# Shifting every buffer of split weights by 192 bytes against the other matmul operands

## What is computed

```
for l in range(2):
    z = rms_norm(x) @ w_in[l]            # 1024 -> 5632: u | q | k | v | two gates
    y_a = s5_branch(u);  y_a = gelu(y_a);  y_a *= sigmoid(y_a @ w_glu[l] + b)
    y_b = rms_norm(diff_attention(rope(q), rope(k), v))
    m = sigmoid(g_ssm) * (y_a @ w_proj_ssm[l]) + sigmoid(g_attn) * (y_b @ w_proj_attn[l])
    x = x + m @ w_out[l]
    h = rms_norm(x)
    x = x + (swiglu(h) if l == 0 else top2_of_8_experts(h))   # hidden width 2816
return rms_norm(x)
```

## Time and profile before

| | before |
|---|---|
| median of 2 runs | 1452.74 us (1451.63 to 1453.85) |
| span of the profiled execution | 1453.1 us |
| TensorE matmul busy (PE) | 1426.3 us, 98% |
| VectorE busy (DVE) | 1179.7 us, 81% |
| ScalarE busy (ACT) | 884.7 us, 61% |
| read from HBM | 390.98 MB |

### The profile page before, as it was taken

The page is one execution under the profiler, slowest core; times in us unless marked ns, Lnnn a source line. Parts: engine busy times, 40 slices in busy tenths (PEclk is TensorE's granted clock), DMA queues, the critical chain, the costliest instruction groups (busy, mean ns, idle before and its releaser), DMA issues.

```text
span 1453.1 us, 22261 instructions
## 1 busy us (share of the span) xinstructions
PE 1426.3 (98%) x8381; PEld 1202.9 (83%) x8381; DVE 1179.7 (81%) x1181; ACT 884.7 (61%) x879; POOL 141.4 (10%) x195
## 2 busy tenths in 40 slices
PE   8999999999999999999999999999999999999997
PEld 6887888999998888887888888888888888888875
DVE  7998886676467697876988988889898898898896
ACT  5334754534344345644768768777777777777774
POOL 1910100000000000101960000000000000000100
PEclk9999999999999999999999999999999999999999
DMA  7443445776455442454999999999999999999993
GB/s 285 136 180 121 156 159 189 261 246 233 151 189 192 174 160 97 151 188 161 365 413 390 406 363 399 380 364 413 353 398 394 354 404 370 379 397 347 419 376 145
DMA packets 94247, 408.87 MB, mean 281 GB/s; under 512 B 28769, under 2 KB 43233, under 8 KB 47714
## 3 DMA queue, kind: packets, MB, share of 16 engines
q1 hardware_dynamic: 75984, 391.37, 69.9%
q10 hardware_dynamic: 17042, 12.36, 2.6%
q0 software_dynamic: 1152, 4.19, 0.7%
HBM read 390.98 MB, written 14.16 MB: 279 GB/s over the span
## 4 chain that ended last, share of the span: by engine, by line
PE 78%; DVE 11%; DMA 3%; SPq 3%; issue 2%; ACT 2%; POOL 1%; DVEq 0%; POOLq 0%; ACTq 0%
PE psum L1938 25%; PE psum L1940 24%; PE psum L1939 24%; DVE w_lo L605 4%; SPq L696 3%; PE psum L1954 2%; DMA w_raw<-in_stream 2%; DMA x_normed<-y_rows,row_number 1%; ACT w_hi L599 1%; ACT square_out L993 0%; PE psum L2284 0%; PE psum L2005 0%; DVE s_r L1511 0%; ACT prob L1129 0%; PE psum L1987 0%
## 5 line engine op out<-in xcount | busy, mean ns | idle before, releaser
L605 DVE TENSOR_TENSOR w_lo<-w_raw,w_hi 128x2048 fp32r<-128x2048 f32 x267 | 607.9, 2293 | 130.2 <-ACT w_hi L599 129.4
L599 ACT ACTIVATE w_hi<-w_raw 128x2048 fp32r<-128x2048 f32 x267 | 509.4, 1915 | 251.1 <-PE psum L1940 191.5
L1938 PE MATMUL psum<-w_hi,hsT_hi 128*128 128x512 f32 x448 | 176.0, 393 | 0.8 <-DVE hsT_lo L1829 0.8
L1940 PE MATMUL psum<-w_lo,hsT_hi 128*128 128x512 f32 x448 | 174.5, 390 | 0.0
L1939 PE MATMUL psum<-w_hi,hsT_lo 128*128 128x512 f32 x448 | 174.3, 389 | 0.0
L1938 PE MATMUL psum<-w_hi,hT_hi 128*128 128x512 f32 x376 | 152.7, 406 | 1.8 <-ACT gate_ssm L1075 1.4
L605 DVE TENSOR_TENSOR w_lo_more<-w_raw,w_hi_more 128x2048 fp32r<-128x2048 f32 x56 | 128.2, 2289 | 24.3 <-ACT w_hi_more L599 23.6
L1940 PE MATMUL psum<-w_lo,hT_hi 128*128 128x512 f32 x376 | 147.4, 392 | 0.0
L1939 PE MATMUL psum<-w_hi,hT_lo 128*128 128x512 f32 x376 | 147.1, 391 | 0.0
L599 ACT ACTIVATE w_hi_more<-w_raw 128x2048 fp32r<-128x2048 f32 x56 | 107.1, 1913 | 21.6 <-DMA w_raw<-in_stream 12.4
L1938 PE MATMUL psum<-hT_hi,w_hi 128*128 128x256 f32 x416 | 116.6, 280 | 0.2 <-DVE hT_lo L1463 0.2
(11 more groups left out here) (429 smaller groups left out, 2651.2 us busy)
## 6 DMA issues: line engine op xcount, KB each, us to landing
w_raw<-in_stream SPq DMA_DIRECT2D x323, 1024.0 KB, 6.9
w_raw_more<-in_stream SPq DMA_DIRECT2D x40, 1024.0 KB, 7.7
h_rows<-one_row ACTq DMA_DIRECT2D x10, 512.0 KB, 6.6
round_rows<-h_rows SPq DMA_DIRECT2D x7, 512.0 KB, 7.0
y_rows<-y_slots ACTq DMA_DIRECT2D x7, 512.0 KB, 9.2
y_rows<-one_row ACTq DMA_DIRECT2D x4, 512.0 KB, 6.2
gain_row<-in_gain_rows SPq DMA_DIRECT2D x3, 512.0 KB
x_tok<-in_x SPq DMA_DIRECT2D x2, 512.0 KB, 6.2
```

Of the source, the lines that this page charges most:

```text
L599: nc.scalar.activation(split_of(seg, i)[0], raw_of(seg, i), ACT.Copy).then_inc(s_hi, 1)
L605: nc.vector.tensor_tensor(l_, raw_of(seg, i), h.bitcast(F32), ALU.subtract).then_inc(s_lo, 1)
L1938: mm(out, lh, rh, start=start, stop=False)
L1940: return mm(out, lh, rl, start=False, stop=stop)
```

## The change

All split weights get the lead, in all segments. `LEAD` becomes a tuple with one entry for each of the five places, all 48. The two places in the mixer's memory start 192 bytes later, and their regions grow by 512 bytes each, which leaves the residues of everything behind them as they were. The raw buffers and all activations stay where they are. No instruction is added, removed or moved on any engine; only addresses differ.

```diff
-LEAD = 48
+LEADS = (48, 48, 48, 48, 48)
...
-        wh = sb("w_hi", [P, NW * SLOT + LEAD], F32R)
+        wh = sb("w_hi", [P, NW * SLOT + LEADS[NW - 1]], F32R)
...
-        a_tab = room(32768)
-        a_rr = room(16384)
+        lead3, lead4 = 4 * LEADS[NW], 4 * LEADS[NW + 1]
+        a_tab = room(32768 + (lead4 + 511) // 512 * 512)
+        a_rr = room(16384 + (lead3 + 511) // 512 * 512)
...
-        whx = [at("w_hi_more0", [P, 1, SLOT], F32R, a_rr), at("w_hi_more1", [P, 1, SLOT], F32R, a_tab + 16384)]
+        whx = [at("w_hi_more0", [P, 1, SLOT], F32R, a_rr + lead3), at("w_hi_more1", [P, 1, SLOT], F32R, a_tab + 16384 + lead4)]
...
-        def stationary(seg, i):
-
-            if seg == 1:
-                return i % NW != 1 and FFN_SLOTS[i][0] != "d"
-            return False
-
         def split_of(seg, i):

             p = i % NW if seg < 3 else ROUND_POS[i]
             if p < NW:
-                a = (p + 2) % NW * SLOT + (LEAD if stationary(seg, i) else 0)
+                a = (p + 2) % NW * SLOT + LEADS[(p + 2) % NW]
                 return wh[:, a:a + SLOT], wl[:, a:a + SLOT]
             return whx[p - NW][:, 0, :], wlx[p - NW][:, 0, :]
```

More of the change, by code:

```diff
@@ L231, in trunk @@
         raw = sb("w_raw", [P, NRAW, SLOT])
-        wh = sb("w_hi", [P, NW * SLOT + LEAD], F32R)
+        wh = sb("w_hi", [P, NW * SLOT + LEADS[NW - 1]], F32R)
         here[0] += (a_hT - here[0]) % 512
-        wl = sb("w_lo", [P, NW * SLOT + LEAD], F32R)
+        wl = sb("w_lo", [P, NW * SLOT + LEADS[NW - 1]], F32R)
         ident = sb("ident", [P, P])
@@ L342, in trunk @@
         rawx = at("w_raw_more", [P, 1, SLOT], F32, a_tab + 8192)
-        whx = [at("w_hi_more0", [P, 1, SLOT], F32R, a_rr), at("w_hi_more1", [P, 1, SLOT], F32R, a_tab + 16384)]
-        wlx = [at("w_lo_more0", [P, 1, SLOT], F32R, a_rr + 8192), at("w_lo_more1", [P, 1, SLOT], F32R, a_tab + 24576)]
+        whx = [at("w_hi_more0", [P, 1, SLOT], F32R, a_rr + lead3), at("w_hi_more1", [P, 1, SLOT], F32R, a_tab + 16384 + lead4)]
+        wlx = [at("w_lo_more0", [P, 1, SLOT], F32R, a_rr + 8192 + lead3), at("w_lo_more1", [P, 1, SLOT], F32R, a_tab + 24576 + lead4)]
         ysh = at("y_slots_hi", [P, D], F32R, a_yh)
```

## The result

The changed kernel takes 1476.62 us (1475.37 to 1477.87, 2 runs) against 1452.74 us before: a ratio of 1.0163, 95% interval 1.0133 to 1.0192. It is 23.9 us slower. That lies outside the forecast range, 1441 to 1462 us, and 3 us short of the rival that the prediction called "slower", 1480 to 1485 us. The span of the profiled execution grew from 1453.1 to 1473.5 us, by 20.4 us. This is 3.5 us less than the runs say; the profiled execution of the changed kernel is 3.1 us shorter than the median of its timed runs, and what follows accounts for the 20.4 us. The interval is 0.3% to either side, so a slowdown of 1.6% is clear of the noise; the prediction was wrong to say that within 2% a measurement of this kernel can hardly tell a change from none.

What follows compares the result with a forecast made beforehand. TensorE was taken to bound the kernel, by its pace per matmul. The terms -0.5 + 0.4 + 0 - 0.5 = -0.6 us, from a median of 1452.74, gave about 1452 us; range 1441 to 1462 us.

Steps and rivals of the forecast that it cites:

- slower: 512-column matmuls: the lead moves load and stream's meeting point into the stream, 5.5 to 6.7 ns each, 1480 to 1485 us; chance 0.12.
- What bounds the kernel: Whole kernel: TensorE, busy 98% of the span; only its nanoseconds per matmul can change on the critical path.
- Weights moving, lead newly given: 4872 matmuls of 512 columns: level operands already on a floor of 226.5 ns, load delays covered; change taken as 0.
- The direction: Moving weights: offset runs opposite to segment 1, stationary operand behind; would decide "slower", but transposes with this direction cost nothing.
- the small gain: Moving weights: lead worth 2.3 ns each as for stationary ones, 11 us gained, 1442 us; chance 0.09.
- Weights stationary, newly given: Block 0, GLU slots and first up slot, 336 matmuls: gain taken as 0.5 us, ends 0 and 2.2.
- Kept: Other 21 gate and up slots, same address relation: two slots at 113.3 ns fall to 117.7, loss of 0.4 us.
- The remainder behind transposes: Some nine uneven distances of 232 ns after transpose sets: lead smooths some, gain taken as 0.5 us, at most some 5.
- The splits: ScalarE and VectorE writing off the raw buffer's residue: still 1.92 and 2.29 us, cost 0.
- The rivals with a gain: Moving weights: large gain, conflict removed, about 1424 us, chance 0.08; small gain, 2.3 ns each, 1442 us, chance 0.09.
- The likeliest case: Whole kernel: the forecast itself, about 1452 us, with 512-column matmuls unchanged in pace; chance 0.71.

Runs made afterwards that it cites:

- two other runs: Changed kernel with stationary activations of the expert rounds shifted too, 1457.61 us; changed kernel loading only 32 of 128 stationary columns in most round matmuls, 1470.32 us.
- the first run: Changed kernel with the expert rounds' stationary activations shifted too, so both operands lie at 320 modulo 512: 1457.61 us, ratio 1.0035.

## Why the prediction was wrong, point by point

**What bounds the kernel** was right. Only the pace of TensorE changed, and nanoseconds times 4872 set the size of the result, though not all of them arrived in the span.

**Weights moving, lead newly given: 0.** This is the step that failed. The argument was that 226.5 ns is a floor, that the level operands are on it, and that a disturbance of the load is hidden at 512 columns. The first two parts held as far as was tried: no distance and no length of load in any kernel measured here gave a steady pace below 226.7 ns. But that something is on its floor says that it can't get better by the change, and says nothing against its getting worse. Nor was the disturbance hidden at 512 columns. The term was 6.6 ns (226.7 to 233.3), and 4872 times that is 32 us, of which 20.4 arrived in the span: 16.7 in seven rounds, 3.6 before them. The rest went into uneven stretches that were slow before, waits of TensorE, the gain of the stationary slots and the longer fall of the clock in the profile of the kernel before.

**The direction** was weighed and then set aside on weak evidence. The prediction named the point, that the offset is the other way round for moving weights, but took the transposes, 108 ns for 111, as a sign that it costs nothing. But 128 columns are a stream of 53 ns at the full clock, half of the 108 ns measured, so something else than the stream sets the pace there, as the prediction itself said of the small gain; they could not show a slower stream of 512 columns. The direction is worth 4.4 ns (228.9 against 233.3), and level operands another 2.2.

**The rival "slower"** had the right sign and nearly the right size: 5.5 to 6.7 ns from two rows of the trace, 6.6 measured. It priced all 4872 matmuls on the path; in the mixers and in the last round waits took up part, so that 1480 to 1485 us became 1476.6. Of its mechanism one half is borne out and one is not. The relation of moving and stationary operand decides, its direction counts, and the cost of the shift is nearly gone beside a short load (0.3 ns). But where the two would meet is not shown, and a short load does not free a level stream (231.4 ns for 226.7). What holds without a picture is the empirical rule by distance modulo 256 bytes. Why a full load beside a level stream gives a better pace than a short one stays open.

**Weights stationary, newly given**: 2.0 ns in block 0 (119.8 to 117.8), 2 to 6 in the GLU slots and 6.6 in the first up slot, some 1.1 us in all, inside the stated ends though twice the 0.5 taken. The 6.6 ns are luck: two other runs with the same addresses there have the first up slot at 117.8. **Kept**: the two fast slots stayed fast and the first gate slot joined them, a gain of 0.2 us where a loss of 0.4 was taken; by the same two runs that is luck too. **The remainder behind transposes** went the other way: nothing was smoothed, the uneven 232 ns became a steady 233.3. **The splits** cost nothing, as forecast: 2.29 us on VectorE and 1.91 on ScalarE in the changed kernel too. That they do not disturb TensorE is shown by the first run and by the distances with both engines idle.

**The rivals with a gain** are refuted: no steady pace fell below 226.7 ns.

**The range and the chances.** The likeliest case got 0.71 on one argument about an unmeasured relation, and slower 0.12. Two of the known facts asked for more: the trace had a 512-column pace of 232 ns in it with the same addresses, so that 226.7 was not unconditional, and the change altered the relation for 4872 matmuls and improved it for 336. A fair range would have reached 1485 us.

## What to carry to other kernels

Keep the moving and the stationary operand of float32 matmuls with 512 moving columns on one residue modulo 256 bytes, exactly; where 256 columns move, 64 or 192 bytes between them are a little better than none (117.8 ns for 120). So the setting goes by the role that a buffer has, not by the buffer. And a pace that is on its floor is a reason to fear a change of its conditions: the bound of such a term is one-sided, with all of the room on the side of loss.

## What the runs showed of the hardware that was not expected

- Start addresses set the pace of TensorE at the full clock: 226.7, 229, 231.7 or 233.3 ns for the same 512-column float32 matmul, by the distance between its operands modulo 256 bytes; 16 bytes are enough to lose 5.0 of the 6.6 ns, 32 lose all. With 256 columns the order is another: 120 ns level, 117.8 at 64 or 192 bytes. At the lower clock level, 1.2 GHz, nothing of this is seen: 427 ns in both kernels.
- A pace is a repeating pattern of distances (232, 226, 229, or 238, 229) that a stream needs a few matmuls to reach after an interruption or a change of distance.
- Loading 32 stationary columns in place of 128 beside a level stream of 512 columns makes the stream slower, 231.4 for 226.7 ns (the output is narrower as well), and beside such loads the relation of the addresses is worth 0.3 ns in place of 6.6.
